# Reordered modulation tiles and loads, a moved b-bar product, wider chunk products and constant products ahead of the first block, in a two-layer hybrid decoder kernel

## The reference, cut to what matters

```python
mod = (c_act @ ada_w[i] + ada_b[i])[:, None, :]       # 1024 x 6144 per layer
sh_m, sc_m, gt_m, sh_f, sc_f, gt_f = jnp.split(mod, 6, axis=-1)
hn = rms_norm(h, norm_mix_w[i]) * (1.0 + sc_m) + sh_m
...
# even_mixer: projection of hn to q, k, v, z, b, a and u, then
o = gated_delta_rule_chunked(q, k, v, g, beta)
y_s5 = s5_layer(u, ...)     # Bb = (exp(Lam dt) - 1)/Lam * B; x_t = Lb x_{t-1} + Bb u_t; y = Re(C x) + D u; GELU; GLU
return jnp.concatenate([o, y_s5], axis=-1) @ w_out
```

## Time and profile before

| | us |
|---|---|
| median of 3 runs | 1443.66 |
| lowest and highest | 1442.03 and 1444.15 |
| the profiled execution | 1442.45 |
| span of its trace | 1440.8 |
| PE busy | 1371.0 (95%) |
| DVE busy | 744.7 (52%) |
| ACT busy | 507.2 (35%) |
| POOL busy | 143.1 (10%) |
| mean granted clock of PE | 0.956 |

### The profile page before, as it was taken

How to read it: one execution, slowest core, us unless ns; L and a number is a source line. 1 busy time by engine, 2 the same in 40 slices (tenths; PEclk the granted TensorE clock), 3 DMA queues, 4 the chain that set the end, 5 groups by cost and what they waited for, 6 DMA issues and landing times.

```text
span 1440.8 us, 17788 instructions
## 1 busy us (share of the span) xinstructions
PE 1371.0 (95%) x6949; PEld 1161.3 (81%) x6949; DVE 744.7 (52%) x801; ACT 507.2 (35%) x586; POOL 143.1 (10%) x216
## 2 busy tenths in 40 slices
PE   6799989989989999999999999999979999999997
PEld 6688878979868888888887888887768888888886
DVE  5889867546664662335654424444483233333343
ACT  5354631251333221223223354664452222122232
POOL 4307985000000000000000000000000000000000
PEclk9799996989989999999999799999989999999999
DMA  9384653511145773345644212111233423343222
GB/s 313 123 143 146 177 145 89 120 57 59 30 146 147 233 233 101 104 116 169 217 124 121 71 59 89 59 44 45 59 87 90 114 74 88 103 116 87 82 75 77
DMA packets 201635, 163.14 MB, mean 113 GB/s; under 512 B 25517, under 2 KB 191626, under 8 KB 199530
## 3 DMA queue, kind: packets, MB, share of 16 engines
q1 hardware_dynamic: 198352, 136.24, 33.4%
q0 software_dynamic: 2720, 25.99, 5.0%
q10 hardware_dynamic: 506, 0.12, 0.1%
HBM read 157.21 MB, written 4.19 MB: 112 GB/s over the span
## 4 chain that ended last, share of the span: by engine, by line
PE 88%; DVE 6%; ACT 3%; issue 2%; DMA 2%; SPq 1%; ACTq 0%; DVEq 0%
PE banks L473 24%; PE banks L475 24%; PE banks L474 24%; PE banks L741 4%; DVE ada_acc L1606 1%; PE banks L1002 1%; PE banks L1029 1%; PE banks L774 1%; PE banks L549 1%; PE banks L738 1%; DMA c_col<-in_c_dram 1%; PE banks L522 1%; PE banks L1020 1%; PE banks L1019 1%; PE banks L776 1%
## 5 line engine op out<-in xcount | busy, mean ns | idle before, releaser
L473 PE MATMUL banks<-hn_hi,whi 128*128 128x512 f32 x992 | 392.6, 396 | 8.6 <-DVE hn_lo L1656 4.9
L474 PE MATMUL banks<-hn_lo,whi 128*128 128x512 f32 x992 | 389.6, 393 | 0.0
L475 PE MATMUL banks<-hn_hi,wlo 128*128 128x512 f32 x992 | 389.4, 393 | 0.0
L1624 DVE TENSOR_TENSOR wlo<-raw,whi 128x2048 fp32r<-128x2048 f32 (+3 forms) x107 | 227.9, 2130 | 129.9 <-ACT whi L1197 69.8
L1203 ACT ACTIVATE whi<-raw 128x2048 fp32r<-128x2048 f32 (+1 forms) x66 | 123.1, 1865 | 314.4 <-PE banks L475 314.2
L473 PEld LDWEIGHTS banks<-hn_hi,whi 128*128 128x128 f32 x992 | 188.7, 190 | 50.8 <-issue 11.4
L475 PEld LDWEIGHTS banks<-hn_hi,wlo 128*128 128x128 f32 x992 | 188.4, 190 | 40.3
L474 PEld LDWEIGHTS banks<-hn_lo,whi 128*128 128x128 f32 x992 | 188.7, 190 | 38.7
L473 PE MATMUL banks<-ff_hi,whi 128*128 128x512 f32 x416 | 164.4, 395 | 0.0
L475 PE MATMUL banks<-ff_hi,wlo 128*128 128x512 f32 x416 | 163.0, 392 | 0.0
L474 PE MATMUL banks<-ff_lo,whi 128*128 128x512 f32 x416 | 163.0, 392 | 0.0
(11 more groups left out here) (435 smaller groups left out, 1776.0 us busy)
## 6 DMA issues: line engine op xcount, KB each, us to landing
raw<-in_ffn_w_in_dram SPq DMA_DIRECT2D x88, 512.0 KB, 4.9
ada_in<-in_ada_w_dram POOLq DMA_DIRECT2D x16, 1536.0 KB, 6.3
ada_in<-in_ada_w_dram SPq DMA_DIRECT2D x32, 512.0 KB, 4.2
raw<-in_ffn_w_out_dram SPq DMA_DIRECT2D x32, 384.0 KB, 4.0
raw<-in_sb_w_in_dram SPq DMA_DIRECT2D x24, 512.0 KB, 4.2
raw<-in_hy_w_in_dram SPq DMA_DIRECT2D x20, 512.0 KB, 6.2
raw<-in_ffn_w_out_dram SPq DMA_DIRECT2D x32, 320.0 KB, 3.6
ada_first<-in_ada_w_dram SPq DMA_DIRECT2D x8, 1024.0 KB, 16.3
```

Of the source, the lines that this page charges most:

```text
L473: pe.matmul(o, lh, rh, start=first, stop=False)
L474: pe.matmul(o, lh, rl, start=False, stop=False)
L475: return pe.matmul(o, ll, rh, start=False, stop=last)
L1624: TTO(wlo[s][:, 0:width], raw[s][:, 0:width], whi[s][:, 0:width].bitcast(F32), SUB)\
```

## The change

Five edits, all ahead of the first layer's output projection.

1. SP: tiles 0 to 7 of part 4 and 0, 1 of part 5 come first, then the stores of y, then tiles 2 and 3, then (after the wait for the stores) the loads of `y_s5`, then tiles 4 to 7.
2. PE: 18 products of constants (`ones` times `ident`, 128 x 128 against 128 columns, fp32, into bank 6, which nobody reads) behind line 599, and 9 behind line 601.
3. PE: in rounds 0 to 6 of y the `m_in` product takes the 64 columns of its own group and the 64 of the next group's input. The second half lands in the columns of the next round, which that round's own product (start=True) writes anew.
4. DVE: the six b-bar products move from ahead of tile 4 to behind `lo(1, 1)`, directly ahead of `w_rows`.
5. DVE: part 4 has 2 tiles instead of 4 ahead of `dec`; from there on every pair stands one place later, and the last pair of part 5 stands behind `x2`.

```diff
@@ sync
-            for part in range(4, 6):
-                for t in range(8):
-                    ada0_tile(part, t)
+            for t in range(8):
+                ada0_tile(4, t)
+            for t in range(2):
+                ada0_tile(5, t)
             for i in range(SC):
                 ...
                 sp.dma_start(y_dram[i].rearrange("(g h) c -> h g c", h=GH),
                              u_rows[i * GH:(i + 1) * GH, :, :]).then_inc(y_out, 16)
+            for t in range(2, 4):
+                ada0_tile(5, t)
             sp.wait_ge(y_out, 128)
             for t in range(4):
                 sp.dma_start(y_s5[:, t, :, :],
                              y_dram[:, t * P:(t + 1) * P, :].rearrange("i p c -> p i c")).then_inc(y_in, 16)
+            for t in range(4, 8):
+                ada0_tile(5, t)
@@ tensor
+            def keep_busy(times):
+                for _ in range(times):
+                    pe.matmul(bank[6][:, 0:P], ones[:, :], ident[:, :], start=True, stop=True)
+
             ...
             last.then_inc(shift_sum, 1)
+            keep_busy(18)
             pe.wait_ge(vec_ready, 1)
             mod_parts(1, ada0_acc[1:2], (16,))
+            keep_busy(9)
@@ tensor, y
-                    yield bank[b][:, r * NC:(r + 1) * NC], slice(64 * par, 64 * par + 64), i, 2 * i + par
+                    yield bank[b][:, r * NC:], slice(64 * par, 64 * par + 64), i, 2 * i + par
             for r in range(8):
+                wide = 2 if r < 7 else 1
                 for o, rows, i, g in lanes(r):
-                    pe.matmul(o, m_in[:, g, :], u_rows[:, g, :], start=True, stop=False)
+                    pe.matmul(o[:, 0:wide * NC], m_in[:, g, :],
+                              u_rows[:, g:g + wide, :].rearrange("p a c -> p (a c)"), start=True, stop=False)
@@ vector
-            dve.wait_ge(bc_in, 16 * 4)
-            (the six b-bar products and their wait)
             ...
             lo(1, 1)
+            dve.wait_ge(bc_in, 16 * 4)
+            (the six b-bar products and their wait)
             w_rows(0, 0)
@@ vector, pairs of tiles in DeltaNet's stages
-            for t in range(4):
+            for t in range(2):
                 ada0_tile(4, t)
             ...                                    # dec, then kt
-            for t in range(4, 6):
+            for t in range(2, 4):
                 ada0_tile(4, t)
             ...                                    # lt, at
-            for t in range(6, 8):
+            for t in range(4, 6):
                 ada0_tile(4, t)
             ...                                    # qdT, lo(10), lo(11)
-            for t in range(2):
-                ada0_tile(5, t)
+            for t in range(6, 8):
+                ada0_tile(4, t)
             ...                                    # l, Da and X
-            for t in range(2, 4):
+            for t in range(2):
                 ada0_tile(5, t)
             onto("x1", X, ADD)
-            for t in range(4, 6):
+            for t in range(2, 4):
                 ada0_tile(5, t)
             ...                                    # d4t
-            for t in range(6, 8):
+            for t in range(4, 6):
                 ada0_tile(5, t)
             onto("x2", X, ADD)
+            for t in range(6, 8):
+                ada0_tile(5, t)
             mod_parts(2, 4)
```

More of the change, by code:

```diff
@@ L1767, in _ @@
             lo(1, 1)
+            dve.wait_ge(bc_in, 16 * 4)
+            f_re = f_co[:, 0, :].unsqueeze(2).to_broadcast([P, PAIRS, GH])
+            f_im = f_co[:, 1, :].unsqueeze(2).to_broadcast([P, PAIRS, GH])
+            t0 = bb_t[:, :, :]
+            step(TTO(t0, b_im[:, :, :], f_im, MUL))
+            step(TTO(bb_re[:, :, :], b_re[:, :, :], f_re, MUL))
+            step(TTO(bb_re[:, :, :], bb_re[:, :, :], t0, SUB))
+            step(TTO(t0, b_re[:, :, :], f_im, MUL))
+            step(TTO(bb_im[:, :, :], b_im[:, :, :], f_re, MUL))
+            TTO(bb_im[:, :, :], bb_im[:, :, :], t0, ADD).then_inc(bb_done, 1)
+            dve.wait_ge(bb_done, 1)
             w_rows(0, 0)
@@ L1943, in _ @@
                 dve.tensor_copy(DaT[:, hd, :, :], src).then_inc(free, 1)
+            for t in range(4, 6):
+                ada0_tile(5, t)
+            onto("x2", X, ADD)
             for t in range(6, 8):
                 ada0_tile(5, t)
-            onto("x2", X, ADD)
             mod_parts(2, 4)
```

## The result

The changed kernel takes 1421.17 us (median of 4 runs, 1417.30 to 1429.34), and the kernel before beside it 1443.58 (4 runs): the ratio is 0.9854 with a 95% interval of 0.981 to 0.9898. Its profiled execution took 1420.99 us with a span of 1419.4, 21.46 less than that of before. The forecast was 1416 in a range of 1409 to 1432.

What follows compares the result with a forecast made beforehand. PE was taken as the bound, except where it stands, runs at low clock or waits for DVE. Gains 2.4 + 5.7 + 11.5 + 8.2 = 27.8 us off 1442.45 give 1414.7, median 1416; own range 1409 to 1423, full range 1409 to 1432.

Steps and rivals of the forecast that it cites:

- Start: From kernel start to the third weight slot: constants and moved b-bar products gain 2.4 us, DVE becoming the bound there.
- Of the 2.4 us all is kept later, since PE is busy up to gr.: Third slot to gr: the start's whole 2.4 us gain survives, because PE is busy throughout.
- as the prediction allowed for in its range: Behind PE's standstill ahead of the third slot: it could lower the clock for dense work, costing up to 1.7 us.
- Tiles ahead of dec: Before dec on DVE: two of four tiles go, so y starts 5.7 us earlier; bounds 4 to 7.
- that rival: Ahead of y: POOL's masks or ACT's drains end last, moved tiles give nothing, 5.7 us missing, 1422; chance 0.07.
- the one with a low clock from the turns to GLU: Turns to GLU: PE's short waits keep the clock low, 19 us worse than before, 1461 or so; chance 0.04.
- a start later than 219: Sign at y's start, expected at about 216.5: beginning later than 219 us would show the prediction wrong.
- Wide products: In y: 128-column m_in products raise the clock to high, 17.6 us instead of 29.1, gaining 11.5 us.
- y stays at 1.2 GHz: Rival in y: clock stays low despite wide products, y takes 31.2 us, total gain 12.6, 1431; chance 0.19.
- From y to GLU: First turn behind y to the GLU product: 37.2 us instead of 45.4, gaining 8.2; bounds 6 to 10.5.
- The constants: At the start: the constant products give PE time DVE doesn't use, since DVE bounds slot 2; no time of its own.
- the slow one: The rival with the clock low from the turns to GLU: 1461 or so, chance 0.04.

Runs made afterwards that it cites:

- u_bbar: Changed kernel with the six b-bar products ahead of tile 4 again: 1416.69 us (4 runs).
- u_noconst: Changed kernel without the 27 products of constants: 1418.78 us (4 runs).
- o_wide: The kernel before with only the 128-column m_in products in y: 1431.79 us (12 runs).
- a_again: The changed kernel itself a second time, unedited, as base for later runs: 1416.78 us (6 runs).
- c_sums: Changed kernel with the column sums as products of 128 columns instead of one: 1411.16 us (6 runs).
- c_both: Changed kernel with 128-column column sums and DVE's lo(2, 0) ahead of w_rows(1, 1): 1408.66 us (6 runs).
- c_fill: Changed kernel with 128-column sums, lo(2, 0) ahead of w_rows(1, 1), and six constant products in the pause ahead of y: 1406.19 us (6 runs).
- c_fill_nc: The kernel c_fill without the 27 products of constants ahead of the first block: 1410.51 us (6 runs).
- N_fill: Changed kernel with 64-column m_in products and six constant products in the pause ahead of y: 1417.18 us (6 runs).
- u_narrow: Changed kernel with y's m_in products back to 64 columns: 1431.41 us (8 runs).

## Why the prediction was right, and where it was not

**Start: 2.4 us forecast, 3.5 measured, of which 0.7 is chance.** Everything from line 597 on began 0.69 us earlier (39.03 for 39.72), and by that the slot's own gain is 2.8. The modulation moved to 47.15 (forecast 48.1), the sums took 1.92, and PE stood for lo(2, 0) as the prediction said. U_bbar and u_noconst show that either of the two edits could be left out: the slot starts at 82.25 or 82.19 then, and gr no later than in the changed kernel.

**The step that failed: "Of the 2.4 us all is kept later, since PE is busy up to gr."** PE was busy, but not at one clock. From the third slot to gr is dense work of fixed length, and 14 traces hold to one sum: 114.7 to 115.1 us, plus half of the time at the low clock.

| kernel | slot to gr | low clock within | rest |
|---|---|---|---|
| before | 115.11 | 0 | 115.1 |
| after | 119.93 | 3.4 + 6.8 | 114.8 |
| o_wide | 119.78 | 3.4 + 6.8 | 114.7 |
| u_bbar | 118.28 | 6.8 | 114.9 |
| a_again | 118.26 | 3.4 + 3.4 | 114.8 |
| c_sums | 116.68 | 3.4 | 115.0 |
| c_both | 115.09 | 0 | 115.1 |

The changed kernel lost 1.7 us (half of 3.4) behind its standstill, as the prediction allowed for in its range, and 3.4 (half of 6.8) at the column sums and behind them, which it had not looked at. Of the ten traces with one-column sums, nine have a low stretch of 3.4 or 6.8 us between 188 and 201.5; the traced execution of before is the one that hasn't. The four traces with 128-column sums have none there, though c_fill and c_fill_nc have one of 3.4 us further on, among the turns.

Six traces have a stretch of 3.4 us between 160 and 171 and not the one at 82 (a_again and c_fill among them). PE in a_again, in order of time:

```profile
161.54 0.95 PE L690 MATMUL banks<-ones,sq 128*128 128x1 f32 x8
...
164.71 0.39 PE L479 MATMUL banks<-hn_lo,whi 128*128 128x512 f32 x1
...
165.27 0.63 PE L478 MATMUL banks<-hn_hi,whi 128*128 128x512 f32 x1
```

In all six the clock falls within 1.3 us of the end of the same 20 records of one and 16 columns (161.54 to 163.84 here). The other eight traces have these records and no fall, and no run changed them, so they are a suspect and not a shown cause.

The prediction took the one execution of before, with no low stretch from slot to gr, as the rule. O_wide has the code of before up to y, and its trace spends 119.78 us there. So much of this loss is no effect of the change but of which execution was traced.

**Tiles ahead of dec: right.** Two rows of DVE, which answer to the earlier trace rows:

```profile
196.62 2.93 DVE L1620 SCALAR_TENSOR_TENSOR ada_acc<-ada_in,c_act,ada_acc 128x1024 f32<-128x1024 f32 x1
202.08 4.23 DVE L1906 TENSOR_SCALAR dec<-banks,gc 128x128 f32<-128x128 f32 x16 [2.53 <-PE banks L762]
```

DVE is free at 199.55, as forecast (199), but gr was late, so dec waits for PE. From dec to y is 17.54 us and was 17.53: everything between kept its length. Measured from gr the term is 6.4. POOL's scan was no bound, so that rival falls; so does the one with a low clock from the turns to GLU, which no trace of the changed kernel shows. Y began at 219.62, not near 216.5, which is the failed step above. The prediction had named a start later than 219 as a sign that it was wrong, and in this execution that sign came; in a_again y began at 218.44.

**Wide products: right in size, wrong in reason.** 17.54 us against 17.6, the largest term. The prediction had wide products raise a low clock, from the rise under the turns at 256 to 260. C_sums refutes this: wide products at 0.50 for 31 us and no rise. Every trace enters y at the high clock, and the question is whether the clock then falls. N_fill shows that narrow y keeps it when the standstill in front is filled, and u_narrow and o_wide that behind the standstill the width makes the fall rarer. So the largest term came out right by luck: no trace shows the rise within y that it was built on. Read by their times, one run in ten of the changed kernel (1429.34, mean granted clock 0.957, the others of that call 0.970 or 0.971) and two in twelve of o_wide had y low, against six in eight of u_narrow and most runs of before; c_sums has two in six. That is read from the times; traced with y low are before, u_narrow and c_sums alone. The rival "y stays at 1.2 GHz" is thus real, in one run in ten. By the Trainium skill (TensorE: Matmul & The Clock Gate, Part 1) the number of matmuls that run at the low clock at a kernel's start varies from run to run of the same kernel. The traces here show such a change further on as well, with a low stretch at 191.3 to 198.2 in one execution of the changed kernel and at 165.0 to 168.4 and 192.3 to 195.8 in another. The same part would have an engine that is busy throughout rise to the high clock, and c_sums, busy 4.00 of 4.00 us at 0.50, disagrees.

**From y to GLU: 4.7 instead of 8.2 us.** The mechanism held: y's stores left right behind y, GELU was at 259.14 (22.0 us behind the first turn, and its rounding ended at 25.8 where 24 was forecast, still ahead of need), and PE no longer waited ahead of x3. The size was off in four pieces. DVE in order of time:

```profile
259.88 2.68 DVE L1620 SCALAR_TENSOR_TENSOR ada_acc<-ada_in,c_act,ada_acc 128x1024 f32<-128x1024 f32 x2 [1.06 <-DMA ada_in<-in_ada_w_dram]
262.48 2.47 DVE L1947 TENSOR_TENSOR X<-X,banks 128x512 f32<-128x512 f32 x4
...
267.92 1.28 DVE L1620 SCALAR_TENSOR_TENSOR ada_acc<-ada_in,c_act,ada_acc 128x1024 f32<-128x1024 f32 x1 [1.77 <-DMA ada_in<-in_ada_w_dram]
```

The tiles of edit 1 that SP loads behind y's loads come late: DVE waits 1.06 us ahead of x2, hence PE's 1.64, of which 0.48 was there before, and 1.77 ahead of the last tile, hence PE's 0.46. The prediction asked whether y_s5 would be in time and not whether the tiles queued behind it would. The third piece is the clock: the two halves of the sums took 4.8 us without their wait, not 3.6. The fourth is DVE at the first products behind the turns: with the turns fast, PE comes to its copies of Da earlier, waits for them (0.26 us in the row at 241.40), and takes 8.12 us from 239.09 to 247.21 where before took 7.18 (257.24 to 264.42). Together 1.16 + 0.46 + 1.17 + 0.94 = 3.73, less 0.2 by which x3 was shorter than forecast: the 3.5 that are missing. That the loads' place makes the tiles late is read from these rows; no run moved it alone.

**The constants** did nothing, as forecast, because DVE bounded the slot; with DVE's bound gone c_fill_nc shows what they are worth otherwise.

**The balance.** 27.8 us forecast, 21.4 traced: 3.7 lost up to gr and 3.5 behind y, 0.8 more than forecast from gr to y's end. The median of the ten runs is 1418.0, 2 from the forecast, which is closer than the terms deserve: in the traced execution 7.2 us of them failed, and it lies 3 us above that median. One sum of the rivals is off by a little: by the reckoning of the others, the slow one gives 1462.7 and not 1461, and nothing rests on it.

**What stays open.** Why the clock falls behind the same pause in some executions and not in others isn't shown, nor what sets off the stretches near 165, beyond the small products that stand ahead of them, nor which of the shorter runs of before (1430 to 1433) had y at the high clock, since one execution per kernel was traced.

## What to carry to other kernels

A standstill of PE can cost more than its length, because the work behind it can run at half clock (y: 1.32 us of standstill, 11.6 us of y). Filling it with products of constants is free where PE would stand anyway, but pays only where PE bounds what follows. Count a gain at the place where it is still there: between the change and the next wait, add half of every low stretch. And where a stage has two times, compare many runs, since one trace shows only one of them.

## What the runs showed that was not expected

- Plain fp32 products of 128 columns cost as much as those of one column, as the prediction had read for 64, and the sums made so leave no low stretch behind them: 3.77 us for 32 records against 1.84 for 16, that is 0.118 and 0.115 us a record.
- PE busy without a gap can stay at 1.2 GHz for 31 us (218.2 to 248.9 in c_sums), with 128-column products among its work.
- Short standstills were enough to be followed by a fall: 1.32 us ahead of y, 1.79 to 2.53 us ahead of the third slot (three traces), while 2.53 us there in a_again and 2.57 in u_narrow had none behind them.
